# Hybrid decoder layer on one Trainium2 core: the MLP's down product by one level of Strassen's method, its activation forms made on GpSimd beside the up product, and the GATE2 sums on VectorE

## What is computed

```
shift1, scale1, gate1, shift2, scale2, gate2 = split(silu(c) @ w_mod + b_mod, 6)
...                                   # mixer: x = x + gate1 * rms_norm(mixed @ w_out)
h = rms_norm(x, g_pre_mlp) * (1 + scale2) + shift2
u = relu(h @ w_mlp_up)                # 2048 -> 8192
y = (u * u) @ w_mlp_down              # 8192 -> 2048
x = x + gate2 * rms_norm(y, g_post_mlp)
```

## Time and profile before

| what | value |
|---|---|
| median of 3 runs | 2351.09 us |
| the profiled execution: its time / its span | 2352.11 us / 2350.3 us |
| granted TensorE clock, mean | 0.986 of 2.4 GHz |
| PE busy | 2274.2 us (97%) |
| DVE busy | 1447.9 us (62%) |
| ACT busy | 895.0 us (38%) |
| POOL busy | 554.6 us (24%) |
| DMA | 391.21 MB, mean 166 GB/s |
| chain that ended last | PE 55%, DVE 2% |

### The profile page before, as it was taken

One profiled execution on the slowest core, in us unless ns is written; L12 is line 12 of the kernel. 1 busy time (PEld: TensorE's weight loads), 2 busy tenths in 40 slices (PEclk: granted clock), 3 DMA queues, 4 the chain that ended last, 5 costly groups with the idle time before them and its releaser, 6 DMA issues.

```text
span 2350.3 us, 33979 instructions
## 1 busy us (share of the span) xinstructions
PE 2274.2 (97%) x13060; PEld 1908.5 (81%) x13060; DVE 1447.9 (62%) x1790; ACT 895.0 (38%) x1187; POOL 554.6 (24%) x344
## 2 busy tenths in 40 slices
PE   5999999999999999989999999999999999999998
PEld 1556687888777788889999999999888888888886
DVE  6749984993247664887777777776544333333335
ACT  4334325222346322754444444444222223222222
POOL 6543334444446000000000000003999200000000
PEclk8999999999999999999999999999999999999999
DMA  8976665333232485333333333335767445444443
GB/s 309 363 290 251 226 231 138 96 93 93 87 119 79 161 318 174 125 117 135 135 134 134 134 134 134 134 134 197 236 214 224 149 153 180 146 135 146 135 123 141
DMA packets 129760, 391.21 MB, mean 166 GB/s; under 512 B 18320, under 2 KB 19984, under 8 KB 117520
## 3 DMA queue, kind: packets, MB, share of 16 engines
q1 hardware_dynamic: 115408, 347.65, 43.0%
q10 hardware_dynamic: 9664, 25.70, 2.8%
q0 software_dynamic: 4608, 16.78, 2.4%
HBM read 356.25 MB, written 33.57 MB: 166 GB/s over the span
## 4 chain that ended last, share of the span: by engine, by line
PE 55%; DVE 2%; issue 0%; ACT 0%; DVEq 0%; ACTq 0%
PE psum L920 19%; PE psum L919 18%; PE psum L921 18%; DVE y L2494 0%; DVE x_in L2512 0%; DVE B_raw L2377 0%; DVE w_lo L2274 0%; DVE T_lo L2361 0%; PE psum L1355 0%; ACT T_hi L1736 0%; DVE B_lo L2361 0%; DVE unit_odd L2293 0%; DVE unit_odd L2296 0%; DVEq L246 0%; ACT w_hi L1682 0%
## 5 line engine op out<-in xcount | busy, mean ns | idle before, releaser
L2301 DVE TENSOR_TENSOR w_lo<-raw,w_hi 128x1024 fp32r<-128x1024 f32 x128 | 176.1, 1375 | 425.1 <-ACT w_hi L1682 425.1
L920 PE MATMUL psum<-w_lo,uin_hi 128*128 128x512 f32 x1024 | 409.5, 400 | 0.0
L919 PE MATMUL psum<-w_hi,uin_hi 128*128 128x512 f32 x1024 | 404.6, 395 | 0.0
L921 PE MATMUL psum<-w_hi,uin_lo 128*128 128x512 f32 x1024 | 402.3, 393 | 0.0
L1682 ACT ACTIVATE w_hi<-raw 128x1024 fp32r<-128x1024 f32 x128 | 135.9, 1061 | 491.5 <-PE psum L921 476.6
L837 POOL TENSOR_TENSOR w_lo<-raw,w_hi 128x1024 fp32r<-128x1024 f32 (+1 forms) x96 | 235.1, 2455 | 355.5 <-ACT w_hi L1386 355.5
L919 PE MATMUL psum<-T_hi,w_hi 128*128 128x256 f32 x1024 | 287.9, 281 | 7.5 <-DVE u_t L2392 5.2
L920 PE MATMUL psum<-T_lo,w_hi 128*128 128x256 f32 x1024 | 287.6, 281 | 0.0
L921 PE MATMUL psum<-T_hi,w_lo 128*128 128x256 f32 x1024 | 287.5, 281 | 0.0
L1386 ACT ACTIVATE w_hi<-raw 128x1024 fp32r<-128x1024 f32 (+1 forms) x128 | 129.4, 1016 | 334.8 <-PE psum L921 293.3
L919 PE MATMUL psum<-h_hi,w_hi 128*128 128x512 f32 (+1 forms) x592 | 239.2, 404 | 14.3 <-issue 9.9
(11 more groups left out here) (327 smaller groups left out, 4403.9 us busy)
## 6 DMA issues: line engine op xcount, KB each, us to landing
raw<-in_w_mlp_down SPq DMA_DIRECT2D x128, 512.0 KB, 3.9
raw<-in_w_in SPq DMA_DIRECT2D x88, 512.0 KB, 3.7
mod_ring<-in_w_mod_first SPq DMA_DIRECT2D x32, 1024.0 KB, 8.8
mod_slab<-in_w_mod SPq DMA_DIRECT2D x32, 1024.0 KB, 5.1
raw<-in_w_up_units SPq DMA_DIRECT2D x64, 512.0 KB, 4.3
unit_odd<-in_w_up_units SPq DMA_DIRECT2D x64, 512.0 KB, 5.0
uin<-u_s SPq DMA_DIRECT2D x128, 256.0 KB, 4.2
raw<-in_w_out SPq DMA_DIRECT2D x32, 512.0 KB, 5.9
```

What stands on the lines that cost most here:

```text
L919: nc.tensor.matmul(o, a_hi, b_hi, start=first, stop=False)
L920: nc.tensor.matmul(o, a_hi, b_lo, start=False, stop=False)
L921: return nc.tensor.matmul(o, a_lo, b_hi, start=False, stop=last)
L2301: V.tensor_tensor(w_lo[:, slot, :, :], raw[:, slot, :, :], w_hi[:, slot, :, :].bitcast(F32), ALU.subtract).then_inc(down_lo, 1)
```

## The change

1. **Down product by Strassen's method.** The inner dimension is cut into four blocks kb of 2048 rows, each in 8 units n (column block c = n // 2, half j = n % 2 of the block's rows). A unit is again four 512 KB quadrants of re-laid weights, four sums and seven products m of 24 matmuls with 256 moving columns: 4 x 8 x 7 x 24 = 5376 matmuls in place of 3072 with 512. Seven banks hold the seven products. After the second half (j = 1) ACT copies product 0 out and DVE makes seven sums of PSUM and SBUF (128x512, `put`); from the second block on POOL adds four of the parts to the result in SBUF (`add_parts`).
2. **Activation forms on POOL.** For each up unit POOL makes T3, T1, T2, T4 (subtractions of two SBUF tiles, 256 wide, each waiting for the one before) and, when ACT has made the high parts of all seven forms (one Copy, 1792 wide), the low parts (one subtraction, 1792 wide). ACT stores both to DRAM in two DMAs; `u_st` has one buffer, not two. In the down product SP loads the forms by 1 MB, 14 per block.
3. **GATE2 on DVE.** The 32 gate slabs are loaded by SP, two with each slab of the groups g9 and g10; DVE does 18 multiply-adds ahead of the sums of squares (L2150) and 14 behind them, before it frees the banks of g10. PE sums the row over partitions behind slab 6 of g11.
4. **End.** Columns 1536 to 2047 are finished last, for all 512 tokens; the gate products of the other columns are POOL's, during the last unit.

```diff
@@ SP, projection: behind load_slab(s + 3) and load_mod @@
+                if GATE_AT <= s < GATE_AT + GATE_HALVES // 2:
+                    load_gate(2 * (s - GATE_AT))
+                    load_gate(2 * (s - GATE_AT) + 1)
...
@@ SP, down @@
+            def load_form(m, j, kb):
+                half = DN_PAIRS // 2
+                sp.wait_ge(op_used, kb * (DN_SUB * OPS) + (N_OPS - (2 - j) * OPS + m + 1))
+                sp.dma_start(b_all[dn_tile(m)][:, :, half * j:half * j + half, :].bitcast(F32),
+                             u2f[:, :, FORMS.index(DN_FORM[m]), bass.ds(kb * DN_PAIRS + half * j, half), :]).then_inc(form_landed[m][j], 16)
...
@@ POOL @@
+            def forms(unit, first=False):
+                pool.wait_ge(u_sq_ready, unit + 1)
+                ch.put(nc.gpsimd.tensor_tensor(uf[:, U_T3, :], uf[:, U_B22, :], uf[:, U_B12, :], ALU.subtract))
+                loop_link(nc.gpsimd.tensor_tensor(uf[:, U_T1, :], uf[:, U_B12, :], uf[:, U_B11, :], ALU.subtract), unit, 1)
+                loop_link(nc.gpsimd.tensor_tensor(uf[:, U_T2, :], uf[:, U_B22, :], uf[:, U_T1, :], ALU.subtract), unit, 2)
+                nc.gpsimd.tensor_tensor(uf[:, U_T4, :], uf[:, U_B21, :], uf[:, U_T2, :], ALU.subtract).then_inc(f_formed, 1)
+                pool.wait_ge(f_formed, unit + 1)
+                pool.wait_ge(f_hi_ready, unit + 1)
+                if not first:
+                    pool.wait_ge(f_stored, unit * 32)
+                nc.gpsimd.tensor_tensor(f_lo[:], uf[:, U_B11:, :], f_hi[:].bitcast(F32), ALU.subtract).then_inc(f_lo_ready, 1)
...
@@ PE @@
+                if j == SG - 2:
+                    pe.wait_ge(gate_step, GATE_HALVES)
+                    for k in range(KD):
+                        last = nc.tensor.matmul(bank(STAGE["g10"], 2)[:, k:k + 1], acc_g[:, P * k:P * k + P], ones[:, 0:1], start=True, stop=True)
+                    last.then_inc(gate_sum, 1)
...
+            def down(n, m, kb):
...
+                pe.wait_ge(op_lo, p + 1)
+                if n < 2:
+                    pe.wait_ge(form_landed[m][j], kb * 16 + 16)
...
+                for k in range(DN_PAIRS // 2):
...
+                    for t in range(2):
...
+                        last = three(o, b_hi[name][:, pair, tok], b_lo[name][:, pair, tok], w_hi[:, slot, a, w:w + TOK],
+                                     w_lo[:, slot, a, w:w + TOK], (j, k, t) == (0, 0, 0), (j, k, t) == (1, DN_PAIRS // 2 - 1, 1))
@@ ACT, up product @@
             def finish_unit(n, i):
...
                 nc.scalar.activation(u, u, ACT.Relu).then_inc(u_relu_ready, 1)
-                act.wait_ge(u_relu_ready, at_ + 1)
-                nc.scalar.activation(u, u, ACT.Square).then_inc(u_sq_ready, 1)
...
-                act.dma_start(to, u_st[n % 2][:]).then_inc(u_stored[n % 2], 16)
+                act.wait_ge(u_relu_ready, unit + 1)
+                if not at_start(i) or n:
+                    act.wait_ge(f_lo_ready, unit)
+                nc.scalar.activation(uf[:, 0:QUADS, :], u, ACT.Square).then_inc(u_sq_ready, 1)
+            def forms_high(n, i):
...
+                nc.scalar.activation(f_hi[:], uf[:, U_B11:, :], ACT.Copy).then_inc(f_hi_ready, 1)
...
+                if m == 0:
+                    finish_unit(n - 1, i)
+                if m == 3:
+                    forms_high(n - 1, i)
+                if m == 6:
+                    store_forms(n - 1, i)
@@ DVE, comb, m == 1 @@
-                        dve.wait_ge(u_stored[n % 2], i * (16 * BLOCK // 2) + (16 * (n // 2)))
+                        dve.wait_ge(u_sq_ready, i * BLOCK + n)
...
@@ DVE, projection @@
+            for q in range(GATE_FIRST):
+                gate_add(q)
             dve.wait_ge(branch_act, BRANCH_SQ)
...
             dve.sem_inc(branch_dve, 1)
+            for q in range(GATE_FIRST, GATE_HALVES):
+                gate_add(q)
```

More of the change, by code:

```diff
@@ new lines, in loop_link, with add_parts @@
+            def loop_link(instruction, unit, nth):
+                instruction.then_inc(t_chain, 1)
+                pool.wait_ge(t_chain, unit * 2 + nth)
+            def add_parts(c, kb, last=False):
+                done = kb * (DN_KEYS * DN_EVICTIONS) + DN_EVICTIONS * c
+                for tokens, side, part, after in ((0, 1, u3_part, 3), (0, 0, x_part, 4), (1, 1, u3_part, 6), (1, 0, u2_part, 7)):
+                    y = y_part(tokens, c, side)
+                    pool.wait_ge(dn_done, done + after)
+                    nc.gpsimd.tensor_tensor(y, y, part[:], ALU.add).then_inc(y_pool, 1)
@@ new lines, in _ @@
+            forms(0, True)
+            with pool.Fori(1, UNITS) as unit:
+                forms(unit)
+            pool.wait_ge(dn_done, DN_KEYS * DN_EVICTIONS)
+            pool.sem_inc(y_pool, 16)
+            with pool.Fori(1, DN_LAST) as kb:
+                for c in range(DN_KEYS):
+                    add_parts(c, kb)
+            for c in range(DN_KEYS - 1):
+                add_parts(c, DN_LAST)
+            pool.wait_ge(g_landed, 48)
+            for c in range(DN_KEYS - 1):
+                pool.wait_ge(y2_squared, TT * c + TT)
+                for t in range(TT):
+                    y = y_row(t, c)
+                    nc.gpsimd.tensor_tensor(y, y, g2_of(c), ALU.mult).then_inc(y_gated, 1)
@@ L907, in _ @@
+            c = DN_KEYS - 1
+            for tokens, side, part, after in ((0, 1, u3_part, 3), (0, 0, x_part, 4), (1, 0, u2_part, 5), (1, 1, u3_part, 6)):
+                y = y_part(tokens, c, side)
+                pool.wait_ge(dn_done, DN_EVICTIONS * (DN_KEYS * DN_LAST + c) + after)
+                nc.gpsimd.tensor_tensor(y, y, part[:], ALU.add).then_inc(y_pool, 1)
         @block.tensor
@@ L1339, in _ @@
-            for j in range(DN_GROUP):
-                down_ready(0, j)
-                for nth, t in enumerate(((2, 0, 3, 1), (0, 2, 1, 3))[TURN_HALF]):
-                    if j == 0:
-                        pe.wait_ge(comb_ready, N_COMBS * UNITS - (6, 4, 1, 0)[nth])
-                    for half in range(2):
-                        last = down(j, t, half, j == 0, False)
-                last.then_inc(down_used, 1)
-            with pe.Fori(1, UK // DN_GROUP - 1) as i:
-                down_group(i)
@@ L1374, in _ @@
+            for n in range(DN_SUB):
+                for m in range(OPS):
+                    down(n, m, 0)
+            with pe.Fori(1, DN_KEYS) as kb:
+                for n in range(DN_SUB):
+                    for m in range(OPS):
+                        down(n, m, kb)
         @block.scalar
@@ L2179, in _ @@
             head_split(1)
+            dve.wait_ge(gate_sum, 1)
+            V.tensor_tensor(mod[:, 5, :], bank(STAGE["g10"], 2)[:, 0:KD], cols("b_mod5"), ALU.add).then_inc(gate_read, 1)
+            dve.wait_ge(gate_read, 1)
+            V.tensor_tensor(mod[:, 5, :], mod[:, 5, :], cols("g_post2"), ALU.mult).then_inc(gate_col, 1)
             done("g11")
```

626 lines of the change are left out of this document (367 added, 259 removed).

## The result

The changed kernel takes 2449.95 us (median of 4 runs, 2449.64 to 2454.82) against 2351.41 of the kernel before: the ratio is 1.0419 (95% interval 1.0395 to 1.0442), 4.2% slower. The forecast was 2432, slower, with a range of 2338 to 2465. The profiled execution has a span of 2447.8 us, 97.5 more than before.

What follows compares the result with a forecast made beforehand. PE was taken to bound both big products, with DVE nearly full in the up product. Terms −86.4 + 151 + 4 + 2 + 10 = +81 us on 2352.1 gave 2433, as median 2432 us; range 2338 to 2465.

Steps and rivals of the forecast that it cites:

- The mechanism: Up product: DVE and POOL subtractions of two SBUF tiles exclude each other for whole instructions, so PE waits; +151 us.
- The forecast's turn: Up product: DVE's time from one unit's last sum to the next, 24.9 us against PE's 19.7.
- the order: Up product: step-by-step schedule of ACT, DVE and POOL through one unit, assuming DVE late; closes at 24.95 us.
- rival 2: Up product: POOL fills DVE's waits, only the lock's own time counts; +66 us, 2347 us; chance 0.14.
- The upper bound of 25.6 us: Up product: DVE's 15.0, its waits of 3.6 and all 7.0 of POOL added for one unit; +173 us.
- Rival 1: Up product: POOL's forms fit into DVE's gaps and PSUM sums, so POOL is hidden; 2281 us; chance 0.16.
- half the columns cost half the time: Down product: 256-column matmuls spaced 0.1173 us against 0.2334 for 512 columns, so Strassen's version saves 86.4 us.
- Rival 3: Down product: it stalls too, at form loads or by POOL's additions; 25 us more, 2458 us; chance 0.08.
- +2 (0 to 15): Turn from up to down product: DMA demand for forms and units, 479 GB/s asked, costs +2 us, range 0 to 15.
- 630 us of PE with no wait; no DMA as releaser: Down product: expected sign that PE runs 630 us without waiting and no wait is ended by DMA.
- Projection, +4 forecast: Ahead of the up product: added gate loads and adds delay low parts and freeing of g10's banks; +4 us (0 to 12).
- the last add is at 646 to 650: Projection: twelve gate slabs after the folds, in pairs, take some 30 us, so DVE's last gate add falls at 646 to 650.

Runs made afterwards that it cites:

- experiment 1: Changed kernel with POOL's T sums and low parts of the forms left out for units 1 to 31; 2341.29 us, ratio 0.9958.
- experiment 6: Changed kernel; values' high parts copied earlier, last four gate adds after the banks are freed, SP holds loads for unit 30's store; 2453.19 us, ratio 1.0406.
- (11): Changed kernel with SP loading only the high parts of the forms in the down product; 2445.63 us, ratio 1.0368.
- (12): Changed kernel; forms' low parts on DVE behind a unit's last sum, values' copies and last gate adds reordered, stores mostly on SP, down-product loop written out; 2326.52 us, ratio 0.9868.
- experiment 9: Changed kernel; forms' low parts on DVE behind a unit's last sum, projection reordered, Relu, Square and first sum later at m = 1; 2365.47 us, ratio 1.0034.
- (10): Kernel of experiment 9 with the token half as outer loop of the down product's matmuls; 2367.54 us, ratio 1.0041.

## Why the prediction was right, and where it was not

**The mechanism was right, its size 1.65 us a turn too large.** The forecast's turn was 24.95 us, the measured one 23.3; experiment 1 shows that all of the excess over 19.71 is POOL. By the forecast's own steps, from the start of the fourth weight sum (1241.21): P1's copy came at 2.7, not 3.45. The two stores cost ACT 0.32 us there, not 1.15, since they were issued while the copy before them ran. ACT's rows:

```profile
1242.54 1.06 ACT L1749 ACTIVATE w_hi<-raw 128x1024 fp32r<-128x1024 f32 x1 [9.96 <-DVE raw L2444]
1242.75 0.38 ACTq L1829 DMA_DIRECT2D u2f<-f_hi  x1
1243.29 0.46 ACTq L1829 DMA_DIRECT2D u2f<-f_lo  x1
1243.92 0.39 ACT L1836 ACTIVATE p_t<-psum 128x256 f32<-128x256 f32 x1 [0.32 <-issue]
```

High part 5 and the T sums came earlier by as much. The rest of the difference is in the price of a T sum: low part 5 was held 0.4 us by the end of T1, and T2 and T4 cost the next two DVE instructions 0.54 us each, where the order had charged all of POOL's 0.73. Low part 6 ended at 10.4, not 11.45, and POOL took the lock for the low part at 13.0 (14.5). From there the order ran as written. Result +109 us for +151, near the middle between the forecast and rival 2 (66). The granted clock in the up product stayed 1.00 with all these waits, as charged. The upper bound of 25.6 us rests on waits of 3.6 us for which the prediction shows no rows; the four measured ones are 2.6.

**Rival 1** (POOL hidden, 2281) is refuted by the waits of 82.9 us in 88 pieces, and **rival 2** (POOL fills DVE's waits) by those waits: all four are still there. POOL's forms come when ACT has caught up, as was said against rival 1.

**The down product was under-costed by 48 us.** The forecast held the spacing of the up product (0.1173) for it; 5376 x 0.0027 = 14.5 us. The step that failed is "half the columns cost half the time", read in one product and carried to another in which the form is the stationary operand. 26.7 us are PE's stalls: 2.7, 11.0 and 3.4 at the first start, 4.4 and 4.2 at two later starts, 1.0 at the end. Behind them the matmuls come slower, at a mean granted clock of 0.78 to 0.83 over the next 9 to 11 us (0.94 over 27.5 us at the first), which makes some 9 us more; 2 of all this had been charged. Rival 3 (25 us, 0.08) named this stage and its form loads. At the first start the shape was right but the victim was ACT: it waits 14.4 us for unit 30's store, 1.8 MB in 1 KB packets among 4 KB packets of the loads (7.5 us when no load runs beside it, experiment 6). The forecast put "+2 (0 to 15)" on this turn and asked only when the loads are due, not who waits for the stores. The sign "630 us of PE with no wait; no DMA as releaser" did not come. The stalls of 4.3 us do not go with half the form bytes (11) and go with PE's loop (12), which the forecast did not cost; the up product's loop, half as long, shows none.

**Projection, +4 forecast, some 14 measured.** The step "the last add is at 646 to 650" failed. The folds ended at 615.7, not 613, and the 14 adds behind them took from 615.9 to 658.1, 3.0 us each, where 33 to 37 us for all were forecast, 2.4 to 2.6 each: SP sends two gate slabs per slab of `w_in` and waits for DVE in between, POOL's low parts stretch some adds from 1.28 us, and SP's lateness holds ACT's high parts of the values. Experiment 6 removed this wait by order alone, and 4.7 us of another came.

**The end** was right to 0.6 us. What is left of the projection is 20.6, less the stall of 11.2 and 2.6 us by which PE came later to it (649.5, not 646.9; no more than that arrival varies from profile to profile), 6.8 us, for a forecast of 6.9. That this fits is partly luck: the gate sums moved to g11 take 3.5 and the matmuls behind them, at lower clock, 1.8 us, together 5.3, and 1.4 us belong to the sums of squares, slower behind the stall.

## What to carry to other kernels

Before GpSimd is given work beside VectorE, count VectorE's instructions with two SBUF inputs: one that meets a GpSimd instruction reading SBUF waits for most or all of it. Here one long piece cost VectorE more (3.86 us) than the same work in seven (2.3), and what took 4.1 us on GpSimd took 2.0 us on VectorE itself. When the fuller engine has waits for another that waits for it in turn, those waits are no slack; work has to be put exactly in them, and whether it fits only a run tells (experiment 9 was plausible and wrong). Of a spill to DRAM, cost both directions, above all who waits for the store when the loads of the next stage start.

## What was not expected of the hardware

- 256-column matmuls follow each other by 0.1173 us in the up product, where it has no waits (before, 1, 12), and by 0.1200 in the Strassen down product of every kernel here, with PE never idle and the clock at 1.00. It is not the loop (12), not the alternation of the target (10), and not POOL, which is idle from 1830 to 1960 us in the changed kernel (1086 matmuls in 130 us). That it is the change of the stationary operand is not shown. It stays open.
- PE lost 4.2 to 4.8 us at each jump back in a loop whose body is 56 x 24 matmuls (1344, each with a weight load), and nothing when it was written out. Why that body and not the up product's (28 x 24, where no two matmuls of the kernel before start more than 0.12 us apart between 1100 and 1500 us) is not shown; no run has a body of another length.
